# A state-space scan decimated by two, its sixteen tiles taken in eight pairs

## The chip, the cores and the metric

The kernel runs on one core of one Trainium2 chip. The metric is device time in microseconds (us) of the whole program, a network of two transformer-like layers and a third block. Everything is in float32.

## The reference, cut to what matters

The change touches one part of the first layer's mixer, the S5 scan. 32 groups of 64 complex states run over 256 time steps:

```python
lb = exp(a * dt)                                   # complex, |lb| = mag
bb = (lb - 1) / a * b                              # 16 inputs -> 64 states
bu = einsum('bsgc,gpc->bsgp', u, bb)
h[t] = lb * h[t-1] + bu[t]                         # by lax.associative_scan
y = real(einsum('bsgp,gcp->bsgc', h, c)) + d_skip * u
att = forgetting_attention(q, k, v, f_logit)       # 8 heads, softmax over 256 keys
y = gelu(y); y = y * sigmoid(y @ w_glu + b_glu)
out = concatenate([att, y]) @ w_out
```

## The kernel before, in words

The program has a thread per engine, written out by hand and held together by semaphores. Weights come in 1 MB units over SyncE's queue into a ring of twelve slots. In the first phase (class `Fox`) four of them are lent out as working memory, so that eight hold weights. Every VectorE, ScalarE and GpSimd instruction waits for the one before it (`Steps`).

In `Fox` the 32 groups are 16 tiles of 128 partitions (two groups of 64 states). Tile j runs through these steps:

- `tile_input` (L801, TensorE): two matmuls of 32 rows and 256 columns make the real and imaginary input in one PSUM bank (`INPUT`, banks 0 and 1).
- `turn_in` (L1155 to L1157, VectorE): the input is multiplied by a table of cosines and sines of -t times the state's angle, so that what is left is a real recurrence. The sum of the two products is GpSimd's (L1177).
- `scan` (L1166, VectorE): two real scans of 256 steps. VectorE turns tile j+1 in ahead of scan j, so that GpSimd's sum runs behind it.
- `turn_back` (L1193, L1194, GpSimd): two products of 512 elements with the table give `by_cos` and `by_sin`.
- `tile_output` (L812 to L815, TensorE): four matmuls of 256 columns, with 32 output columns each, one beside the other in the array's column groups.
- `keep_turn` (L835, ScalarE) copies the result, and after every fourth tile `tile_sums` (L824, TensorE) folds four of them, again side by side, into the output y; `y_keep` adds the skip term.

The table (256 columns for each of 16 tiles) is built by VectorE by doubling; ScalarE mirrors its half (`mirror`). TensorE meanwhile makes the products of u, q and k, and the product of v between the first tiles. Then a loop over tiles 3 to 15 follows on every engine. Behind eight of the tiles (`HEAD_BEHIND`) one attention head each is done: `turn_p` (L598), `head_out` (L606, L608) and `scores` (L588, L790) on TensorE, maxima on VectorE, exponentials on ScalarE. TensorE issues `tile_input(j + 4)` at the end of iteration j:

```python
for j in range(3, 16):
    self.tile_output(pe, j)
    ...
    if 7 <= j + 4 < 16:
        self.tile_input(pe, j + 4)
```

After the loop comes the product with the output weights (`mix_part`, L946), the GLU and the layer norm.

Of the kernel before, what the change touches and what calls it, by code (L numbers as in the profile page):

```python
# [12 lines left out]
ACT = mybir.ActivationFunctionType  # L13
# [4 lines left out]
P = 128  # L18
SEQ = 256
# [329 lines left out]
class Start(Phase):  # L349
# [36 lines left out]
    def sync_second(self, sp):  # L386

        net, io, fox = self.net, self.net.io, self.net.phase_objects[1]
        for n, dst in enumerate(fox.C):
            sp.dma_start(dst, io["s5_c"][n].rearrange("p (k n) -> p k n", k=16)).then_inc(fox.s("params_loaded"), 16)  # L390
# [335 lines left out]
class Fox(Residual, Heads):  # L726
# [5 lines left out]
    HEAD_BEHIND = {5: 0, 6: 1, 8: 2, 9: 3, 10: 4, 12: 5, 13: 6, 14: 7}  # L732
# [4 lines left out]
    def __init__(self, net):  # L737
# [3 lines left out]
        self.uT = a.take(4 * SEQ, 4, SEQ)  # L741
# [4 lines left out]
        self.Cz = [a.take(512, 16, 32) for _ in range(2)]  # L746
        self.ut = a.take(1024)
        self.g = [self.ut[:, 0:512], self.ut[:, 512:1024], a.take(512)]
        self.t = a.take(512)
        self.w = a.take(20 * 16, 20, 16)  # L750
        self.ph = [a.take(16 * SEQ, 16, SEQ) for _ in range(2)]

        b = Arena(net.ring, self.LENT * UNIT)
        odd = [b.take(512) for _ in range(2)]
        self.C = [h.rearrange("p (a b) -> p a b", a=16) for h in odd]
        self.alloc_heads(b)
        self.sel = b.take(8 * P, 8, P, rows=8)
        self.ft = [b.take(SEQ, rows=8) for _ in range(6)]
        self.c_rows = b.take(16, NT, 8)
        self.strips = [b.take(SEQ) for _ in range(3)] + [a.take(SEQ)]  # L760
        self.f_strips = self.strips[0]
        self.turned = [[b.take(512) for _ in range(2)], odd]
        self.yT = self.catT[:, 4:8, :]
        self.mask = net.causal[:, :]
        self.sig = [self.B[0].rearrange("p a b -> p (a b)"), self.B[1].rearrange("p a b -> p (a b)")]

# [29 lines left out]
    def tile_input(self, pe, j):  # L796

        k, m = divmod(j, 4)
        t = self.net.T.open(pe, ("bu", j), self.INPUT)
        for part in range(2):  # L800
            mm = pe.matmul(t[:, part * SEQ:(part + 1) * SEQ], self.B[part][32 * m:32 * m + 32, k, :],  # L801
                           self.uT[32 * m:32 * m + 32, k, :], start=True, stop=True)
        self.net.T.close(("bu", j), mm)

    def tile_output(self, pe, j):

        T = self.net.T
        t = T.open(pe, ("turn", j), self.TURN)
        pe.wait_ge(self.s("h_ready"), j + 1)
        by_cos, by_sin = self.turned[j % 2]  # L810
        re, im = slice(0, SEQ), slice(SEQ, 2 * SEQ)
        pe.matmul(t[0:32, re], self.Cz[0][:, j, :], by_cos[:, re], start=True, stop=True, skip_group_check=True)  # L812
        pe.matmul(t[32:64, re], self.Cz[1][:, j, :], by_cos[:, im], start=True, stop=True, skip_group_check=True)
        pe.matmul(t[64:96, re], self.Cz[1][:, j, :], by_sin[:, re], start=True, stop=True, skip_group_check=True)
        T.close(("turn", j), pe.matmul(t[96:128, re], self.Cz[0][:, j, :], by_sin[:, im], start=True, stop=True,  # L815
                                       skip_group_check=True))

    def tile_sums(self, pe, k):

        T = self.net.T  # L820
        t = T.open(pe, ("y", k), self.SUMS)
        pe.wait_ge(self.s("turn_kept"), 4 * k + 4)
        for m in range(4):
            mm = pe.matmul(t[32 * m:32 * m + 32, 0:SEQ], self.net.fold[:, 0:32], self.strips[m], start=True, stop=True,  # L824
                           skip_group_check=True)
        T.close(("y", k), mm)

    def keep_turn(self, act, j):

        net, T = self.net, self.net.T  # L830
        k, m = divmod(j, 4)
        if k:
            T.take(act, ("y", k - 1))
        t = T.take(act, ("turn", j))
        net.ac(act.activation(self.strips[m], t[:, 0:SEQ], ACT.Copy, scale=self.w[:, 19, 0:1]))  # L835
        T.free(act, ("turn", j))
        act.sem_inc(self.s("turn_kept"), 1)

    def tensor(self, pe):
# [5 lines left out]
        pe.wait_ge(self.s("params_loaded"), 16 * 4)  # L845
        pe.wait_ge(self.s("u_kept"), 4)
        for j in range(2):
            self.tile_input(pe, j)
# [4 lines left out]
        self.tile_input(pe, 2)  # L853
        vs = [net.use_unit(pe) for _ in range(2)]
        t = T.open(pe, ("fox_v", 0), rest)
        net.part(pe, t, vs, net.xT, 0, range(4))
        self.tile_input(pe, 3)
        self.tile_output(pe, 0)
        T.close(("fox_v", 0), net.part(pe, t, vs, net.xT, 0, range(4, KT)))
        self.tile_input(pe, 4)  # L860
        self.tile_output(pe, 1)
        t = T.open(pe, ("fox_v", 1), rest)
        net.part(pe, t, vs, net.xT, 1, range(4))
        self.tile_input(pe, 5)
        self.tile_output(pe, 2)
        T.close(("fox_v", 1), net.part(pe, t, vs, net.xT, 1, range(4, KT)))
        net.release([u for u, _ in vs], ("fox_v", 1))
        self.tile_input(pe, 6)
        pe.wait_ge(self.s("c_ready"), 1)
# [7 lines left out]
        for j in range(3, 16):  # L877
            self.tile_output(pe, j)
            if j == 3:
                self.scores(pe, 1)  # L880
# [2389 lines left out]
```

## Time and profile before

| what | value |
|---|---|
| median of 3 runs | 1944.28 us (1937.16 to 1944.61) |
| the profiled execution's own time | 1941.67 us |
| its span, first to last instruction | 1939.5 us |
| TensorE busy | 1799.3 us, 93% of the span |
| VectorE, ScalarE, GpSimd busy | 563.7, 371.9, 209.9 us |
| mean granted TensorE clock | 0.961 |

A profile shows one execution. Times are us from the span's start. "Busy" leaves out waits; the rows of a timeline merge neighbours of a kind (x4), and in brackets stands how long the engine was idle before. PEld is the loading of weights into TensorE's array. In float32 a matmul of the program shows as two MATMUL records, so that "x4" of L801 is one tile's two matmuls. Where matmuls follow one another, the difference of two starts is the time that the first took; the durations themselves overlap.

### The profile page before, as it was taken

Reading aid. Unit: us, or ns where it says so; the run is one execution under the profiler, and the core shown is the slowest. Engines: PE = TensorE matmul, PEld = TensorE weight load, DVE = VectorE, ACT = ScalarE, POOL = GpSimd, SP = SyncE. Lnnn points to the kernel's source line nnn. Section 1 sums busy time; section 2 is a strip of 40 time slices with the busy share of each in tenths; the row PEclk is TensorE's granted clock in tenths of the full one; section 3 lists DMA queues with packets and bytes.
Section 4 is the critical chain, followed back from the end, with each engine's and each line's share of the span. In section 5 each row is a group of like instructions: output and inputs, shape, how many; then the busy total and the mean of one; then the engine's idle time right before and its main releaser. Section 6 shows DMA issues by size and latency. Waiting matters only on the chain.

```text
span 1939.5 us, 21648 instructions
## 1 busy us (share of the span) xinstructions
PE 1799.3 (93%) x6956; PEld 934.2 (48%) x6957; DVE 563.7 (29%) x1236; ACT 371.9 (19%) x679; POOL 209.9 (11%) x403
## 2 busy tenths in 40 slices
PE   8998799899989989999989999999999988888886
PEld 6444333486633337855865475444443333232332
DVE  8882500587650031431372221011140000000002
ACT  1233311222221111032241100111032111110101
POOL 0561122000002310000000000000001110110100
PEclk9858899999989989999999999999999999999998
DMA  9002499676428993323413344332357999999995
GB/s 376 23 1 97 187 377 422 262 278 243 174 89 321 422 405 133 149 111 141 174 55 123 131 158 151 153 130 98 144 226 293 422 422 422 422 422 422 422 422 248
DMA packets 70439, 468.82 MB, mean 242 GB/s; under 512 B 7848, under 2 KB 12112, under 8 KB 15072
## 3 DMA queue, kind: packets, MB, share of 16 engines
q1 hardware_dynamic: 66016, 457.56, 58.1%
q10 hardware_dynamic: 4352, 10.35, 1.6%
q8 instruction: 40, 0.66, 0.1%
q14 instruction: 31, 0.25, 0.0%
HBM read 466.82 MB, written 1.06 MB: 241 GB/s over the span
## 4 chain that ended last, share of the span: by engine, by line
PE 67%; DMA 18%; DVE 10%; issue 2%; ACT 2%; SPq 0%; POOL 0%; DVEq 0%; ACTq 0%; POOLq 0%
PE bank L255 18%; DMA ring_sb<-stream 17%; PE bank L268 13%; PE bank L2705 10%; PE bank L1667 4%; PE bank L2748 4%; PE bank L2715 4%; PE bank L2642 2%; DVE scratch_sb L1027 2%; PE bank L301 2%; PE bank L946 1%; PE bank L1945 1%; DVE scratch_sb L1166 1%; DMA scratch_sb<-before 1%; PE bank L1302 1%
## 5 line engine op out<-in xcount | busy, mean ns | idle before, releaser
L2705 PE MATMUL bank<-ring_sb,scratch_sb 128*64 128x512 f32 x1536 | 347.3, 600 | 55.0 <-DMA ring_sb<-stream 48.8
L268 PE MATMUL bank<-xT_sb,ring_sb 128*128 128x256 f32 x1216 | 264.3, 379 | 0.0
L2705 PEld LDWEIGHTS bank<-ring_sb,scratch_sb 128*64 128x64 f32 x1536 | 115.4, 138 | 282.3 <-issue 273.2
L268 PEld LDWEIGHTS bank<-xT_sb,ring_sb 128*128 128x128 f32 x1216 | 230.6, 190 | 33.5 <-issue 2.5
L255 PE MATMUL bank<-ring_sb,xT_sb 128*128 128x512 f32 x416 | 179.4, 592 | 0.0
L255 PE MATMUL bank<-ring_sb,scratch_sb 128*128 128x512 f32 x384 | 167.7, 598 | 7.3 <-ACTq L2309 3.9
L2748 PE MATMUL bank<-ring_sb,scratch_sb 128*64 128x512 f32 x768 | 171.9, 596 | 0.0
L2866 DVE TENSOR_TENSOR scratch_sb<-scratch_sb,bank 128x256 f32<-128x256 f32 (+1 forms) x32 | 17.7, 554 | 408.9 <-PE bank L2705 278.7
L255 PEld LDWEIGHTS bank<-ring_sb,xT_sb 128*128 128x128 f32 x416 | 78.9, 190 | 97.7 <-issue 97.6
L2715 PE MATMUL bank<-scratch_sb 128*128 128x512 f32 x256 | 123.7, 606 | 0.0
L255 PEld LDWEIGHTS bank<-ring_sb,scratch_sb 128*128 128x128 f32 x384 | 73.1, 191 | 98.5 <-issue 90.6
L2982 ACT ACTIVATE scratch_sb<-bank 128x256 f32<-128x256 f32 (+1 forms) x96 | 47.1, 491 | 379.6 <-PE bank L2730 203.1
L2910 POOL COPY scratch_sb<-scratch_sb 128x256 f32 x128 | 45.2, 397 | 537.9 <-PEq L2608 525.7
L2871 DVE COPY scratch_sb<-bank 128x512 f32<-128x512 f32 x32 | 22.1, 692 | 277.7 <-PE bank L2748 277.7
L2748 PEld LDWEIGHTS bank<-ring_sb,scratch_sb 128*64 128x64 f32 x768 | 52.3, 137 | 96.8 <-issue 96.8
L1667 PE MATMUL bank<-ring_sb,xT_sb 128*128 128x512 f32 x192 | 84.5, 592 | 0.0
L2918 POOL TENSOR_SCALAR scratch_sb<-iota_sb,scratch_sb 128x64 f32<-128x64 f32 x128 | 71.7, 578 | 0.2
L2715 PEld LDWEIGHTS bank<-scratch_sb 128*128 128x128 f32 x256 | 43.5, 190 | 56.6 <-issue 56.6
L1667 PEld LDWEIGHTS bank<-ring_sb,xT_sb 128*128 128x128 f32 x192 | 36.3, 190 | 42.0 <-issue 41.6
L2985 ACT ACTIVATE scratch_sb<-bank 128x256 f32<-128x256 f32 (+1 forms) x32 | 15.7, 491 | 202.3 <-PE bank L2705 202.3
L2642 PE MATMUL bank<-scratch_sb 128*128 128x512 f32 x96 | 47.9, 663 | 6.8 <-DVEq L2813 6.8
L1361 DVE SCALAR_TENSOR_TENSOR scratch_sb<-ring_sb,mod_sb,scratch_sb 128x512 f32<-128x512 f32 x56 | 42.1, 752 | 2.9 <-DVE scratch_sb L667 0.2
(405 smaller groups left out, 1743.9 us busy)
## 6 DMA issues: line engine op xcount, KB each, us to landing
ring_sb<-stream SPq DMA_DIRECT2D x432, 1024.0 KB, 10.8
rows_sb<-rows ACTq DMA_DIRECT2D x12, 512.0 KB, 4.8
xT_sb<-xT SPq DMA_DIRECT2D x2, 512.0 KB, 7.1
x_sb<-x SPq DMA_DIRECT2D x1, 1024.0 KB, 19.9
scratch_sb<-bias_by_distance ACTq DMA_DIRECT2D x1, 1024.0 KB, 5.3
out<-x_sb ACTq DMA_DIRECT2D x2, 512.0 KB, 2.6
scratch_sb<-decay ACTq DMA_DIRECT2D x1, 768.0 KB, 5.4
small_sb<-small SPq DMA_DIRECT2D x1, 640.0 KB, 13.7
```

Source lines behind the costliest of these rows:

```text
L255: mm = pe.matmul(t[:, :], actT[:, k, i * P:(i + 1) * P], w[:, k % 4, :], start=k == 0, stop=k == kt - 1)
L268: mm = pe.matmul(t[:, m * SEQ:(m + 1) * SEQ], w[:, k % 4, n0:n0 + P], actT[:, k, :], start=k == 0, stop=k == kt - 1)
L301: mm = pe.matmul(bank[:, :], actT[:, k, i * P:(i + 1) * P], w[:, k % 4, :], start=k == 0, stop=k == kt - 1)
L1361: net.dv(dve.scalar_tensor_tensor(part, w[:, k, :], c, part, ALU.mult, ALU.add))
L1667: mm = pe.matmul(self.gate_bank[:, :], net.xT[:, kk, i * P:(i + 1) * P], w[:, k, :], start=kk == 0, stop=kk == KT - 1)
L2642: return pe.matmul(bank[:, :], self.src[:, i, k * P:(k + 1) * P], self.pick[i], start=i == 0, stop=i == 1)
L2705: mm = pe.matmul(t[e * TILE:(e + 1) * TILE, :], self.xs[e][:, kk, :], ws[e][:, k, :], start=kk == 0, stop=kk == KT - 1, skip_group_check=True)
L2715: pe.matmul(T.bank[2 * i + c][:, :], self.scatter[:, i * P:(i + 1) * P], self.y[:, c * 512:(c + 1) * 512], start=False, stop=False, skip_g ...
L2748: mm = pe.matmul(T.bank[6 + c][e * TILE:(e + 1) * TILE, :], self.hidT[:, ff, e * TILE:(e + 1) * TILE], ws[e][:, f, c * 512:(c + 1) * 512], ...
L2910: pool.tensor_copy(self.xs[e][:, 4 * m:4 * m + 4, :], self.xg[:, 4 * m:4 * m + 4, bass.ds(at[e] + tile * TILE, TILE)])\
L2918: pool.tensor_scalar(self.weigh[:, i, e * TILE:(e + 1) * TILE], self.net.iota[:, tile * TILE:(tile + 1) * TILE], self.of_pair[:, 0, i, e:e ...
L2982: act.activation(out, src, ACT.Copy).then_inc(self.tile_sem(f"freed{b}", over), 1)
```

## The change

Every second step of the recurrence is left out: h[2n+1] follows from h[2n-1] with lb squared and the input lb*b*u[2n] + b*u[2n+1]. So a scan runs over 128 steps and gives the odd times. The output at odd times is C h as before, and at even times it is (C lb) h[2n-1] plus a direct term K0 u[2n] with K0 = C b. Two tiles that were of 256 steps are taken together as a pair with the same 512 elements.

- New weights: lb*b (`lag`), C (`Cz`) and C lb (`E`) are computed by VectorE in a compact form (16 columns for each tile, in place of 32), spread by ScalarE into block form (`spread`, 16 instructions), and TensorE turns lb*b by 32 matmuls (`lag_weights`) and computes K0 by 32 matmuls of 32x32 (`direct_weights`). `lag_weights` stands ahead of q's product and waits for the spread, `direct_weights` behind it.
- The table has 128 columns for each tile, so the doubling has one round fewer.
- `turn_in`, the sum and `turn_back` work on a pair with the element counts of a tile before. `scan` is four scans of 128 in place of two of 256.
- `pair_input` is 8 matmuls of 128 columns, all on the same 32 rows; `pair_output` 16 matmuls of 128 columns; `pair_sums` is done for every pair: two matmuls of 256 and two of 128 columns, all into the same 32 output partitions.
- In the loop `pair_input(p + 2)` stands ahead of the head in iteration p.
- The s5 parameters come in six transfers in place of four, with the same bytes.

```diff
-    HEAD_BEHIND = {5: 0, 6: 1, 8: 2, 9: 3, 10: 4, 12: 5, 13: 6, 14: 7}
+    HALF = SEQ // 2
+    MID = SEQ // 4
+    HEADS_BEHIND = ((), (0,), (1,), (2,), (3,), (4,), (5,), (6, 7))
...
+    def pair_input(self, pe, p):
+
+        t = self.net.T.open(pe, ("bu", p), self.INPUT)
+        for odd in range(2):
+            k, m = self.tile(p, odd)
+            rows = slice(32 * m, 32 * m + 32)
+            for part in range(2):
+                at = (2 * odd + part) * self.HALF
+                out = t[:, at:at + self.HALF]
+                pe.matmul(out, self.LB[part][rows, k, :], self.uT[rows, k, 0, :], start=True, stop=False,
+                          skip_group_check=True)
+                mm = pe.matmul(out, self.B[part][rows, k, :], self.uT[rows, k, 1, :], start=False, stop=True,
+                               skip_group_check=True)
+        self.net.T.close(("bu", p), mm)
...
+        for odd in range(2):
+            k, m = self.tile(p, odd)
+            rows = slice(32 * m, 32 * m + 32)
+            pe.matmul(t[rows, odd * SEQ:(odd + 1) * SEQ], self.net.fold[:, 0:32],
+                      self.strips[p % 2][:, odd * SEQ:(odd + 1) * SEQ], start=True, stop=False, skip_group_check=True)
+            mm = pe.matmul(t[rows, odd * SEQ:odd * SEQ + self.HALF], self.K0[rows, k, :], self.uT[rows, k, 0, :],
+                           start=False, stop=True, skip_group_check=True)
...
+        self.lag_weights(pe)
         pe.wait_ge(net.sem("strips_kept"), 1)
         net.small_T(pe, "fox_f", self.f_strips, 0, banks=rest)
         net.product_T(pe, "fox_q", net.xT, banks=rest)
+        pe.wait_ge(self.s("params_loaded"), 16 * 6)
+        pe.wait_ge(self.s("u_kept"), 4 + 2)
+        for p in range(2):
+            self.pair_input(pe, p)
+        self.direct_weights(pe)
         net.product_T(pe, "fox_k", net.xT, banks=rest)
...
+        for p in range(2, 8):
+            self.pair_output(pe, p)
+            self.pair_sums(pe, p - 1)
+            if p + 2 < 8:
+                self.pair_input(pe, p + 2)
+            for h in self.HEADS_BEHIND[p]:
+                self.turn_p(pe, h - 1)
                 if h >= 2:
                     self.head_out(pe, h - 2)
                 if h + 2 < HEADS:
                     self.scores(pe, h + 2)
...
         self.turn_in(dve, 0)
+        for p in range(8):
+            if p + 1 < 8:
+                self.turn_in(dve, p + 1)
+            self.scan(dve, p)
```

TensorE in the loop before, an iteration with a head (L812 to L815 the tile's output, L598 `turn_p`, L588 and L790 `scores`, L801 the input of the tile four further on):

```order
L812 MATMUL bank<-ring_sb,scratch_sb 32x256 [waits fox_h_ready,bank3_freed]
L813 MATMUL bank<-ring_sb,scratch_sb 32x256
L814 MATMUL bank<-ring_sb,scratch_sb 32x256
L815 MATMUL bank<-ring_sb,scratch_sb 32x256
L598 MATMUL bank<-ident_sb,ring_sb 128x128 [waits bank7_freed,head_p_ready]
L598 MATMUL bank<-ident_sb,ring_sb 128x128 x2
L588 MATMUL bank<-scratch_sb 128x128 [waits bank4_freed]
L790 MATMUL bank<-ring_sb 128x128
L588 MATMUL bank<-scratch_sb 128x256
L790 MATMUL bank<-ring_sb 128x256
L801 MATMUL bank<-scratch_sb 128x256 [waits bank0_freed]
L801 MATMUL bank<-scratch_sb 128x256
```

And now, iteration 3 up to the middle of the pair's input (L873 `pair_output`, L886 and L888 `pair_sums`, L852 and L854 `pair_input(5)`), which ends ahead of the head:

```order
L873 MATMUL bank<-ring_sb,scratch_sb 32x128 [waits fox_h_ready,bank3_freed]
L873 MATMUL bank<-ring_sb,scratch_sb 32x128 x15
L886 MATMUL bank<-ring_sb,fold_sb 32x256 [waits fox_turn_kept]
L888 MATMUL bank<-scratch_sb 32x128
L886 MATMUL bank<-ring_sb,fold_sb 32x256
L888 MATMUL bank<-scratch_sb 32x128
L852 MATMUL bank<-scratch_sb 128x128 [waits bank1_freed]
L854 MATMUL bank<-scratch_sb 128x128
L852 MATMUL bank<-scratch_sb 128x128
L854 MATMUL bank<-scratch_sb 128x128
```

The input moved from four tiles ahead, behind the head, to two pairs ahead, in front of it, and the sums stand in every iteration.

VectorE now, from the turn-in of a pair (L1268 to L1270; `bank0_ready` is its input from TensorE) to the scans of the pair before it (L1284):

```order
L1268 TENSOR_TENSOR scratch_sb<-bank,scratch_sb 128x512 [waits vector_steps,fox_cleared,fox_h_ready,bank0_ready,fox_table_ready]
L1269 TENSOR_TENSOR scratch_sb<-bank,scratch_sb 128x2x128 [waits vector_steps]
L1270 SCALAR_TENSOR_TENSOR scratch_sb<-bank,scratch_sb 128x2x128 [waits vector_steps]
L1284 SCALAR_TENSOR_TENSOR scratch_sb<-scratch_sb 128x128 [waits vector_steps,fox_cleared]
L1284 SCALAR_TENSOR_TENSOR scratch_sb<-scratch_sb 128x128 [waits vector_steps] x3
```

The scans of pair p stand behind the turn-in of pair p+1, as those of tile j did behind tile j+1.

## Rows read from the trace of the kernel before

**Rows 1.** The page's first line.
```profile
span 1939.5 us, 21648 instructions
```

**Rows 2.** Busy time by window: PE, PEld, DVE, ACT, POOL, then granted clock, DMA share, GB/s.
```profile
57.90:85.50 27.60, 27.56 (x94) 12.00 (x94) 22.53 (x28) 4.15 (x7) 19.80 (x16) 0.88 0.07 28
85.50:143.50 58.00, 55.22 (x213) 28.12 (x210) 48.30 (x79) 21.95 (x59) 34.66 (x28) 0.50 0.00 1
143.50:161.30 17.80, 12.30 (x66) 5.53 (x64) 8.44 (x16) 9.74 (x27) 7.43 (x6) 0.69 0.01 1
```

**Rows 3.** SyncE's queue in order of time: start, duration, instruction.
```profile
25.25 176.11 SPq L3019 DMA_DIRECT2D ring_sb<-stream  x17
```

**Rows 4.** VectorE in order of time: start, duration, line, shapes, idle before.
```profile
56.18 0.69 DVE L1155 TENSOR_TENSOR scratch_sb<-bank,scratch_sb 128x512 f32<-128x512 f32 x1 [0.22 <-DVE ring_sb L1028]
...
69.40 0.69 DVE L1155 TENSOR_TENSOR scratch_sb<-bank,scratch_sb 128x512 f32<-128x512 f32 x1 [0.25 <-DVE scratch_sb L1166]
...
70.59 0.42 DVE L1157 SCALAR_TENSOR_TENSOR scratch_sb<-bank,scratch_sb 128x256 f32<-128x256 f32 x1
71.26 2.80 DVE L1166 TENSOR_TENSOR_SCAN scratch_sb<-scratch_sb 128x256 f32<-128x256 f32 x2 [0.24 <-DVE scratch_sb L1157]
```

**Rows 5.** GpSimd in order of time, the same tile.
```profile
70.63 1.26 POOL L1194 TENSOR_TENSOR ring_sb<-scratch_sb 128x512 f32<-128x512 f32 x1
72.08 1.43 POOL L1171 TENSOR_TENSOR scratch_sb<-scratch_sb 128x512 f32<-128x512 f32 x1 [0.18 <-POOL ring_sb L1194]
```

**Rows 6.** The scan's line: shortest, median, longest of its 32 instructions in ns.
```profile
L1166 DVE TENSOR_TENSOR_SCAN scratch_sb<-scratch_sb x32: 691/1208/1809, 61.7 to 152.8; 128x256 f32<-128x256 f32 x32
```

**Rows 7.** TensorE in order of time, at the full clock.
```profile
71.30 1.12 PE L801 MATMUL bank<-scratch_sb 32*128 32x256 f32 x4
72.36 0.40 PE L812 MATMUL bank<-ring_sb,scratch_sb 128*32 128x256 f32 x1
...
82.87 0.48 PE L588 MATMUL bank<-scratch_sb 64*128 64x128 f32 x2
83.28 0.48 PE L790 MATMUL bank<-ring_sb 8*128 8x128 f32 x2
```

**Rows 8.** TensorE in order of time, at half the clock.
```profile
130.30 0.90 PE L598 MATMUL bank<-ident_sb,ring_sb 128*128 128x128 f32 x3
131.13 1.12 PE L606 MATMUL bank<-ring_sb,scratch_sb 128*64 128x256 f32 x2
...
132.60 0.79 PE L588 MATMUL bank<-scratch_sb 64*128 64x128 f32 x2
133.33 0.79 PE L790 MATMUL bank<-ring_sb 8*128 8x128 f32 x2
...
137.20 0.64 PE L812 MATMUL bank<-ring_sb,scratch_sb 128*32 128x256 f32 x1
...
138.21 2.07 PE L801 MATMUL bank<-scratch_sb 32*128 32x256 f32 x4
140.21 0.64 PE L812 MATMUL bank<-ring_sb,scratch_sb 128*32 128x256 f32 x1
...
141.06 0.65 PE L824 MATMUL bank<-ring_sb,fold_sb 128*32 128x256 f32 x3
...
142.08 0.90 PE L598 MATMUL bank<-ident_sb,ring_sb 128*128 128x128 f32 x3
```

**Rows 9.** The chain that ended last: start, duration, what.
```profile
59.39 6.61 PE bank L301 x8
...
72.99 3.63 PE bank L301 x8
...
161.34 9.42 PE bank L946 x18
```

**Rows 10.** TensorE in order of time, the products of q and k.
```profile
27.75 27.89 PE L268 MATMUL bank<-xT_sb,ring_sb 128*128 128x256 f32 x128
```

**Rows 11.** ScalarE in order of time, the copy ahead of the added spreads.
```profile
26.29 0.38 ACT L288 ACTIVATE ring_sb<-bank 128x256 f32<-128x256 f32 x1 [0.65 <-PE bank L281]
```

More of the change, by code:

```diff
@@ L818, in tile_sums @@
-    def tile_sums(self, pe, k):
-        T = self.net.T
[L821 to L828, printed above, removed]
-        net, T = self.net, self.net.T
[L831 to L836, printed above, removed]
+            t = T.open(pe, ("lag", part), self.STATE)
@@ new lines, in pair_sums @@
+    def pair_sums(self, pe, p):
+        T = self.net.T
+        key = ("y", p // 4)
+        t = T.bank[T.jobs[key][0]] if p % 4 else T.open(pe, key, self.SUMS)
+        pe.wait_ge(self.s("turn_kept"), p + 1)
+        for odd in range(2):
+            k, m = self.tile(p, odd)
+            rows = slice(32 * m, 32 * m + 32)
[3 more added lines that the diff above has]
+                           start=False, stop=True, skip_group_check=True)
+        if p % 4 == 3:
+            T.close(key, mm)
@@ L851, in tensor @@
         net.product_T(pe, "fox_q", net.xT, banks=rest)
-        net.product_T(pe, "fox_k", net.xT, banks=rest)
[L853 to L868, printed above, removed]
+        pe.wait_ge(self.s("params_loaded"), 16 * 6)
[3 more added lines that the diff above has]
+        self.direct_weights(pe)
+        net.product_T(pe, "fox_k", net.xT, banks=rest)
+        self.pair_input(pe, 2)
         pe.wait_ge(self.s("c_ready"), 1)
@@ L873, in tensor @@
         T.close("fox_cT", mm)
-        pe.wait_ge(self.s("qkv_kept"), 6)
+        pe.wait_ge(self.s("qkv_kept"), 4)
         pe.wait_ge(self.s("sel_loaded"), 16)
         self.scores(pe, 0)
[L877 to L880, printed above, removed]
-            if j % 4 == 0:
-                self.tile_sums(pe, j // 4 - 1)
-            if j in self.HEAD_BEHIND:
-                h = self.HEAD_BEHIND[j]
-                if h >= 1:
-                    self.turn_p(pe, h - 1)
+        vs = [net.use_unit(pe) for _ in range(2)]
+        t = T.open(pe, ("fox_v", 0), rest)
+        net.part(pe, t, vs, net.xT, 0, range(4))
+        self.pair_output(pe, 0)
+        self.scores(pe, 1)
+        T.close(("fox_v", 0), net.part(pe, t, vs, net.xT, 0, range(4, KT)))
+        self.pair_input(pe, 3)
+        t = T.open(pe, ("fox_v", 1), rest)
+        net.part(pe, t, vs, net.xT, 1, range(4))
+        self.pair_output(pe, 1)
+        T.close(("fox_v", 1), net.part(pe, t, vs, net.xT, 1, range(4, KT)))
+        net.release([u for u, _ in vs], ("fox_v", 1))
+        self.pair_sums(pe, 0)
+        self.scores(pe, 2)
+        pe.wait_ge(self.s("qkv_kept"), 6)
+        for p in range(2, 8):
[5 more added lines that the diff above has]
+                self.turn_p(pe, h - 1)
                 if h >= 2:
@@ L1167, in scan @@
+    def scan(self, dve, p):
+        n = self.HALF
+        dve.wait_ge(self.s("cleared"), 1 + p + 1)
+        for odd in range(2):
+            for part in range(2):
+                at = (2 * odd + part) * n
+                xs = self.g[p % 3][:, at:at + n]
+                j = 4 * self.tile(p, odd)[0] + p % 4
+                mag = self.w[:, 0, j:j + 1].to_broadcast([P, n])
+                self.net.dv(dve.tensor_tensor_scan(xs, mag, xs, 0.0, ALU.mult, ALU.add))
         dve.sem_inc(self.s("g_ready"), 1)
@@ L1183, in turn_back @@
[L1183 to L1194 removed]
+        po = self.net.po
@@ new lines, in gpsimd, with turn_back @@
+        self.turn_back(pool, 7)
+    def turn_back(self, pool, p):
+        net, T, n = self.net, self.net.T, self.HALF
+        cr, ci = (table[:, self.tiles(p), :].unsqueeze(2).to_broadcast([P, 2, 2, n]) for table in self.ph)
+        g = self.pair_of(self.g[p % 3])
+        u, t = (v[:, :, 1:n + 1].rearrange("p (o a) n -> p o a n", o=2) for v in self.turned[p % 2])
+        pool.wait_ge(self.s("g_ready"), p + 1)
+        if p >= 2:
+            T.take(pool, ("turn", p - 2))
+        net.po(pool.tensor_tensor(u, g, cr, ALU.mult))
+        net.po(pool.tensor_tensor(t, g, ci, ALU.mult))
```

364 lines of the change are left out of this document (210 added, 154 removed).

## The prediction

> **What bounds the kernel now.** I read the page first, then the windows of the first 358 us, the chain of waits up to there, and the timelines of TensorE, VectorE, GpSimd and ScalarE in the first phase. The phase ends with the product that starts at 161.34 [rows 9]. From the first turn-in at 56.18 [rows 4] to the last scan behind 152.8 [rows 6] the chain runs through VectorE's turn-ins and scans. A scan alone takes 0.69 us and 1.81 us where GpSimd's sum runs beside it [rows 6], so work that lies side by side on the two engines is paid one after the other. TensorE is nearly as full: 55.22 of the 58 us from 85.5 to 143.5, at a granted clock of 0.50 [rows 2], the lower of its two levels (1.2 of 2.4 GHz). That is what the reader should see: VectorE sets the end, but TensorE is a few per cent behind it. The DMA queues do nothing in this phase (share 0.00 in the window); SyncE's queue stands from 25.25 for 176 us until slots come back [rows 3]. So whatever the phase gains or loses moves all that follows by the same amount, and nothing absorbs it.
>
> **What the change takes from VectorE and GpSimd.** A pair has the element counts of one tile, so there are 8 turn-ins, sums and turn-backs in place of 16, and scans half as long. If these engines still set the end, some 40 us would go. The work that prepares it (19 products on compact weights, one round of doubling less) ends near where it does now; TensorE's cover for it is over 15 us, since by the sum below it asks for the first pair's turn-back only at about 85, and that is ready near 76. I cost it at nothing. If that cover were gone, the path would be TensorE's K0, ScalarE's logarithm and the table's mirror, and the first turn-in would come 5 to 10 us later than now.
>
> **What it costs TensorE, one matmul at a time.** The stream of a 256-column matmul is 27.89/64 = 0.44 us at the full clock [rows 10], so 128 columns take 0.22, and 0.44 at half. An input matmul of 32 rows and 256 columns takes 1.06/2 = 0.53 [rows 7] and 2.00/2 = 1.00 at half [rows 8]. With 128 columns only the stream halves, which leaves 0.31 and 0.56; a 128-column matmul on 64 rows takes 0.41 [rows 7] and 0.73 [rows 8]. I take 0.36 and 0.62, so `pair_input` costs 8 x that, 2.9 and 5.0 us; the bounds are 0.27 and 0.41 (full), 0.50 and 0.73 (half). `pair_output` has the streams of two tile outputs, 0.63 each (72.36 to 72.99) [rows 7, 9] and 0.85 at half (140.21 to 141.06) [rows 8]: 1.1 and 1.9 with the change of shape; bounds 0.9 to 1.3 and 1.7 to 2.2. `pair_sums` is the part that loses most. Before, four folds ran side by side in 1.02 us for four tiles [rows 8]; now two folds (0.85 to 1.0 each at half) and two K0 matmuls (0.5 to 0.73) stand one behind the other for each pair: 2.9, and 1.7 at the full clock, bounds 2.7 to 3.4. A head is as before: from 130.30 to 132.60 `turn_p` and `head_out` 2.3, and scores 4.6 - 1.0 = 3.6, since 4.6 us to the next output hold an input of 2.0 of which part runs beside the scores [rows 8]; 5.9 in all at half, 3.4 at the full clock.
>
> **Ahead of the loop.** `lag_weights` waits for eight spreads behind 26.29 + 0.38, each 0.38 and a handover [rows 11]: 30.1. Lag matmuls 2.5 (bounds 1.8 and 3.5), the small product 0.6, q's product 13.95 (half of rows 10): 47.2. Two inputs, one at each clock, 7.9, and 32 tiny matmuls, 64 records at between 0.03 and 0.13 us, 4: 59.1. k's product 13.95 and 3 more, because dense work after sparse work starts at half the clock: v's first part took 6.61 where a later one took 3.63 [rows 9]. That is 76.1, against 55.6 now. The third input, the transpose and scores 0: 5.3, v in four parts 14.6 and again 3.0, two outputs 2.2, one sum 1.7, the fourth input 2.9, scores 1 and 2 4.2: the loop starts at 110.0.
>
> **The loop.** Here the change adds a wait. `pair_output(p+1)` needs scan p+1, which stands on VectorE behind the turn-in of pair p+2, and that needs `pair_input(p+2)`, which TensorE ends only in iteration p. From its end: handover 0.1, turn-in 1.6 (69.40 to 71.01), 0.24 to the scan [rows 4], four scans of 0.42 (0.69 shortened in proportion, with a fixed part of 0.16) and one of them held 1.12 by the sum [rows 6], 0.1 between each two and behind them in total 0.2, turn-back 2 x 1.26 and the gap [rows 5], 0.2 to TensorE: 7.8 us. The head of 5.9 runs meanwhile, so TensorE stands for 2 us in each iteration; queued behind its wait are the sums, the next input and the next head, and VectorE waits for that input. Iteration 2 up to its input is 1.9 + 2.9 + 5.0 = 9.8, to 119.8. Three more periods of 7.8 + 9.8 = 17.6 make 172.6. Then 7.8, output and sums 4.8, head 5.9, output and sums 4.8, two heads without scores 4.6, the last 2.3 and sums 2.9: 205.7. Outputs, sums and transposes alone gave the clock back in this trace (0.69 on average after 143.5) [rows 2], so I take off 3: 202.7, against 161.34. The phase is 41 us longer. Against the profiled execution's own 1941.67 us (span 1939.5 [rows 1]) that is **1983 us**. The median of the runs shown is 2.6 us above that execution; I leave the difference in the range.
>
> **A rule against the trace.** TensorE is busy 95% of the window 85.5 to 143.5 and yet has half the clock [rows 2]. The Trainium skill ("TensorE: Matmul & The Clock Gate", section "Why this matters for your kernels") says that a TensorE kept continuously busy gets the full clock. By the trace the loop stays at half, and the sum is 1983; by the rule TensorE would run it at full and the sum would be the first rival's. The measurement decides here, since this loop has the same kinds of small matmuls, and waits besides.
>
> **The rivals.**
> - Full clock: the two inputs and the three dense starts lose no time to the clock (110.0 becomes 101.9), 5.7 up to the input, three periods of 7.8 + 5.7, then 7.8 and 14.6: 170.5, or 9 us longer, **1951 us**. For it: 0.88 in the window with v's product [rows 2]. Against it: each period would have 4 us of standing still, and the loop before had 0.50 with almost none.
> - The other side, faster: the full clock throughout and weights loaded entirely behind streams, so that only columns count (pair input 1.75, output 0.9, sums 1.3). It decides at 0.22 us for a 128-column matmul. The loop starts at 93.7, comes to its input at 97.7, three periods of 7.4 + 3.95 make 131.7, and 7.4 and 13 end it at 152.1: 9 us shorter, **1932 us**. Against it: no row has a 128-column matmul with 128 columns of weights under 0.41. The 40 us of VectorE and GpSimd can't be had even so, as TensorE's own work alone ends here.
> - Dearer: inputs at 0.73 (0.8 more for each of six), sums 3.4, the tiny matmuls 8, half the clock also in the v stretch and at the end: 17 us more, **2000 us**.
>
> **How the numbers follow.** The forecast has 0.66, full clock 0.16, faster 0.06, dearer 0.12. The forecast's own range, from the bounds of the matmuls, is 1966 to 1996. With the full-clock case and most of the dearer one it is 1950 to 2004, which leaves out about 0.16. A measurement of this kernel can tell about 0.5% (10 us) from no change: below 1934.6 or above 1954. Faster 0.05 (most of the third case), the same 0.11 (the better part of full clock and the rest of the third), slower 0.84.
>
> **What the profile after should show.** The first L268 product ends near 47, the second near 76; L301 ends near 105; the loop's L873 groups come about 17 us apart at clock 0.50, each behind a wait for GpSimd of 1 to 3 us; VectorE's L1268 waits for TensorE's bank; eight L852 and L854 matmuls take 4.5 to 5.5 us; the mix product starts near 203. Prices under 0.3 us for L852 at full clock, or a clock near 1 in the loop, would make the forecast wrong; so would L873 without waits.

## The result: 0.55% slower, and the profile after

The changed kernel takes 1950.41 us in the median of seven runs (1948.42 to 1954.28), the kernel before 1941.78 (1936.27 to 1944.61) on the same chip: a ratio of 1.0055 (95% interval 1.0038 to 1.0072), 8.6 us more. The forecast was 41 us more, 1983 us; the measured time lies at the very edge of the range of 1950 to 2004. The profiled execution took 1949.64 us, its span is

```profile
span 1947.9 us, 22251 instructions
```

The windows of [rows 2] with the same columns, and a fourth up to the mix product:

```profile
57.90:85.50 27.60, 27.60 (x141) 18.47 (x140) 11.33 (x22) 2.92 (x5) 8.85 (x7) 0.94 0.11 39
85.50:143.50 58.00, 50.73 (x333) 29.60 (x332) 25.17 (x50) 17.68 (x45) 15.17 (x12) 0.74 0.00 1
143.50:161.30 17.80, 15.97 (x114) 9.09 (x113) 11.36 (x26) 7.54 (x20) 6.32 (x5) 0.71 0.01 2
161.30:175.40 14.10, 9.33 (x33) 4.08 (x31) 0.20 (x2) 5.72 (x15) 0.00 (x0) 0.64 0.00 0
```

From 85.5 to 143.5 VectorE went from 48.30 to 25.17 us and GpSimd from 34.66 to 15.17: the gain that the change aims at is there and lies beside the path. TensorE fell only from 55.22 to 50.73, at a granted clock of 0.74 where it was 0.50. (The window holds v's product at the full clock as well; in the three periods of the loop from 110.82 to 151.91 the clock is 0.62.) The chain that ended last (start, duration, what) has the products of q, k and v and then the mix product, at 161.34 before [rows 9]:

```profile
33.86 14.62 PE bank L268 x64
...
52.88 15.34 PE bank L268 x64
...
72.28 5.33 PE bank L301 x8
...
175.50 7.92 PE bank L1005 x18
...
231.18 16.61 PE bank L2763 x32
...
250.13 8.75 PE bank L2826 x32
```

So the phase is 14.2 us longer. One period of the loop on TensorE, in order of time, from one `pair_output` to the next:

```profile
124.52 1.93 PE L873 MATMUL bank<-scratch_sb 128*32 128x128 f32 x32 [1.89 <-POOLq L1316]
126.25 1.06 PE L886 MATMUL bank<-ring_sb,fold_sb 128*32 128x256 f32 x2
127.24 0.40 PE L888 MATMUL bank<-scratch_sb 32*32 32x128 f32 x2
127.57 0.62 PE L886 MATMUL bank<-ring_sb,fold_sb 128*32 128x256 f32 x2
...
128.45 0.48 PE L852 MATMUL bank<-scratch_sb 32*128 32x128 f32 x2
128.78 0.38 PE L854 MATMUL bank<-scratch_sb 32*128 32x128 f32 x2
129.00 0.38 PE L852 MATMUL bank<-scratch_sb 32*128 32x128 f32 x2
...
130.43 0.75 PE L599 MATMUL bank<-ident_sb,ring_sb 128*128 128x128 f32 x3
...
138.24 1.93 PE L873 MATMUL bank<-ring_sb,scratch_sb 128*32 128x128 f32 x32 [1.85 <-POOLq L1316]
```

Output 1.7 us, sums 2.2, input 2.0, then 7.8 from the end of the input to the next output, of which the head fills 5.9 and 1.85 is a wait for GpSimd. The clock changes twice in each period: the output and the first fold at half, the second fold and the input at full (starts 0.22 apart), the head at half again. The chain that fills the 7.8 us, on VectorE and then GpSimd, here in front of the output at 110.82, is the one forecast:

```profile
103.13 0.69 DVE L1268 TENSOR_TENSOR scratch_sb<-bank,scratch_sb 128x512 f32<-128x512 f32 x1 [4.84 <-PE bank L854]
103.86 0.42 DVE L1269 TENSOR_TENSOR scratch_sb<-bank,scratch_sb 128x256 f32<-128x256 f32 x1
104.32 0.42 DVE L1270 SCALAR_TENSOR_TENSOR scratch_sb<-bank,scratch_sb 128x256 f32<-128x256 f32 x1
104.98 2.91 DVE L1284 TENSOR_TENSOR_SCAN scratch_sb<-scratch_sb 128x128 f32<-128x128 f32 x4 [0.24 <-DVE scratch_sb L1270]
```
```profile
104.97 1.26 POOL L1299 TENSOR_TENSOR scratch_sb<-scratch_sb 128x512 f32<-128x512 f32 x1 [11.11 <-DVEq L1272]
108.03 1.26 POOL L1314 TENSOR_TENSOR ring_sb<-scratch_sb 128x512 f32<-128x512 f32 x1 [1.79 <-DVEq L1285]
109.37 1.26 POOL L1315 TENSOR_TENSOR ring_sb<-scratch_sb 128x512 f32<-128x512 f32 x1
```

Two more stretches of TensorE, ahead of q's product and the tail:

```profile
29.38 3.64 PE L817 MATMUL bank<-ident_sb,scratch_sb 128*32 128x128 f32 x64 [4.59 <-ACTq L1079]
...
162.77 0.38 PE L609 MATMUL bank<-ring_sb,scratch_sb 128*64 128x128 f32 x2
166.28 0.90 PE L599 MATMUL bank<-ident_sb,ring_sb 128*128 128x128 f32 x3 [3.12 <-ACTq L705]
...
170.29 0.90 PE L599 MATMUL bank<-ident_sb,ring_sb 128*128 128x128 f32 x3 [1.65 <-ACTq L705]
...
172.60 1.06 PE L886 MATMUL bank<-ring_sb,fold_sb 128*32 128x256 f32 x2
```

The lag weights wait 4.59 us for ScalarE's spreads, and behind the last pair two heads wait 3.12 and 1.65 us for ScalarE's weights, with the last sums behind them.

### The profile page after: what moved, and what is told of

It is laid out like the page before. It is cut to its first block, busy times and chain, and to the rows that moved or that the text cites. A ratio compares the mean times of both kernels' runs of the same rounds, so it can differ in the third digit from the quotient of the medians.

```text
span 1947.9 us, 22251 instructions
## 1 busy us (share of the span) xinstructions
PE 1800.3 (92%) x7308; PEld 945.5 (49%) x7309; DVE 528.5 (27%) x1218; ACT 376.2 (19%) x690; POOL 181.3 (9%) x384
## 3 DMA queue, kind: packets, MB, share of 16 engines
HBM read 466.82 MB, written 1.06 MB: 240 GB/s over the span
## 4 chain that ended last, share of the span: by engine, by line
PE 71%; DMA 17%; DVE 6%; ACT 2%; issue 2%; POOL 1%; SPq 0%; ACTq 0%; DVEq 0%; POOLq 0%
PE bank L255 18%; DMA ring_sb<-stream 17%; PE bank L268 14%; PE bank L2826 10%; PE bank L1788 4%; PE bank L2869 4%; PE bank L2836 4%; PE bank L2763 2%; PE bank L301 2%; PE bank L1005 1%; PE bank L2066 1%; PE bank L1423 1%; PE bank L995 1%; PE bank L589 1%; PE bank L873 1%
## 5 line engine op out<-in xcount | busy, mean ns | idle before, releaser
L2826 PE MATMUL bank<-ring_sb,scratch_sb 128*64 128x512 f32 x1536 | 345.8, 597 | 56.0 <-DMA ring_sb<-stream 49.8
L2826 PEld LDWEIGHTS bank<-ring_sb,scratch_sb 128*64 128x64 f32 x1536 | 114.6, 137 | 282.3 <-issue 273.5
L2763 PE MATMUL bank<-scratch_sb 128*128 128x512 f32 x96 | 44.6, 624 | 6.8 <-DVEq L2934 6.8
```

Of the source, the lines that this page charges most:

```text
L2763: return pe.matmul(bank[:, :], self.src[:, i, k * P:(k + 1) * P], self.pick[i], start=i == 0, stop=i == 1)
L2826: mm = pe.matmul(t[e * TILE:(e + 1) * TILE, :], self.xs[e][:, kk, :], ws[e][:, k, :], start=kk == 0, stop=kk == KT - 1, skip_group_check=True)
```

## Experiments

Two theories. **Order:** the phase is longer because the change puts waits on TensorE: behind its own `pair_input(p+2)` in each iteration (3.52 + 1.89 + 1.85 + 1.83 = 9.1 us), for the spreads, and in the tail. **Clock:** TensorE's own work is the bound, and the waits only give it the clock that it would not have without them. A third was whether the prices of small matmuls explain it. All edits are against the changed kernel; ratios are against the kernel before, run on the same chip. Experiments 6, 7 and 10 have one execution each, so only their profiles are read.

**1. The input ahead of the output.**
```diff
 for p in range(2, 8):
+    if p + 2 < 8: self.pair_input(pe, p + 2)
     self.pair_output(pe, p)
     self.pair_sums(pe, p - 1)
-    if p + 2 < 8: self.pair_input(pe, p + 2)
```


> In the loop pair_input(p+2) is issued ahead of pair_output(p) in place of behind pair_sums(p-1). Theory A (order): the change costs time since TensorE waits in each iteration for a chain of 7.9 us that starts at the end of its own pair_input. The four waits in front of pair_output(3) to (6), 3.52 + 1.89 + 1.85 + 1.83 = 9.1 us, go, the mix product starts near 166.4 in place of 175.5 and the time falls by about 9 us. Theory B (clock): the waits are what gives TensorE its clock back; without them the loop runs at half, pair_input takes 4.0 us in place of 2.0 and the sums 2.9 in place of 2.2, so each period is about 14.6 in place of 13.7 us and the time rises by 3 to 4 us.

Ratio 1.0005 (0.9984 to 1.0026), a median of 1939.23 us within 1930.17 to 1949.61, and the mix product starts at 161.04. The waits for GpSimd that are left are 0.40 and 0.95 us. The clock did not fall:
```profile
85.50:143.50 58.00, 56.65 (x407) 34.52 (x405) 34.86 (x71) 22.75 (x59) 21.56 (x17) 0.82 0.00 1
```
Moving one call took 14.5 us off the phase and undid the slowdown. The waits account for 7.7 us of it (9.1 less the 1.35 left); most of the rest is the better clock (0.76 in place of 0.67 from the loop's first output to the mix product), which the order theory had not foreseen. The clock theory's loss did not come.

**2. The input between output and sums.**
```diff
     self.pair_output(pe, p)
-    self.pair_sums(pe, p - 1)
     if p + 2 < 8: self.pair_input(pe, p + 2)
+    self.pair_sums(pe, p - 1)
```


> In the loop pair_input(p+2) is issued between pair_output(p) and pair_sums(p-1); the same matmuls, only that the 2.2 us of sums now lie inside the chain of 7.9 us in place of ahead of it. Theory A: in each period the sums fill the wait: 1.85 us less three times and 2.2 once, 7.8 us less, with the waits for GpSimd down to nothing or a few tenths. Theory B: the input, now right behind the output at half the clock, takes 4 us in place of 2, and the gain is gone: within 1 us of the changed kernel.

Ratio 1.0087 (1.0072 to 1.0101), by the ratios 6 us slower than the changed kernel, though the two intervals touch at 1.0072; mix product at 175.67, as the clock theory expected. The waits are gone in the loop after its first, and the clock went with them; the whole period of 14.7 us (121.59 to 136.31) is dense and at half (0.50 in it):
```profile
85.50:143.50 58.00, 54.52 (x323) 32.29 (x322) 25.19 (x51) 17.68 (x45) 15.20 (x12) 0.66 0.00 1
```
```profile
121.59 1.94 PE L873 MATMUL bank<-scratch_sb 128*32 128x128 f32 x32
123.45 0.79 PE L852 MATMUL bank<-scratch_sb 32*128 32x128 f32 x2
...
127.16 1.06 PE L886 MATMUL bank<-ring_sb,fold_sb 128*32 128x256 f32 x2
...
130.27 0.90 PE L599 MATMUL bank<-ident_sb,ring_sb 128*128 128x128 f32 x3
...
136.31 1.08 PE L873 MATMUL bank<-ring_sb,scratch_sb 128*32 128x128 f32 x16
```
The input takes 3.7 us here in place of 2.0. The clock theory is right for this order; the order theory's 7.8 us were all eaten. Taking waits away is worth only what the clock leaves of it. Why the clock rose with the order of experiment 1 and fell with this one, no run shows.

**3. The input's matmuls twice** (pairs 4 to 7, each sum written a second time).
```diff
-        for odd in range(2):
+        for odd in (0, 1, 0, 1) if p >= 4 else (0, 1):
```


> The eight matmuls of pair_input are issued twice for pairs 4 to 7 (the second set writes the same sums again). Both theories: the work stands ahead of the chain, so all of it is paid: 1.75 us by the measured spacing of 0.22 us, four times, 7 us more. If weight loads were the price of these matmuls it would be over 8 us; at half the clock 14 us.

Ratio 1.0116 (1.0098 to 1.0134), some 12 us over the changed kernel in place of 7. The added matmuls start 0.22 us apart until the clock falls inside the second set, and the sums ahead of it take 2.9 us in place of 2.2: a period of 16.8 (112.52 to 129.33), 3.1 more for 1.75 of work at the full clock. The last of the four periods had its whole input at half and took 19.7 us, and the mix product of this execution, the slowest of the four (1968.99; the others 1960.31 to 1964.58), starts at 196.44. So work ahead of the chain is paid in full, and the clock adds to it.

**4. The transposes three times** (heads 0 to 4).
```diff
-        for b in range(3):
+        for b in list(range(3)) * (3 if self.tag == "fox" and g < 5 else 1):
```


> turn_p issues its three transposes three times for heads 0 to 4, some 1.4 us more of TensorE's work at half the clock in each iteration 2 to 6 (one of them, in iteration 2, ahead of the 3.5 us wait), all behind pair_input. Theory A: TensorE stands idle there for 1.8 us or more, so nothing is paid: within 1 us of the changed kernel, and the waits for GpSimd shrink to about 0.4. If TensorE's own work were the bound and the waits only seeming, five times 1.4, 7 us more.

The mix product starts at 174.71 (175.50 in the changed kernel), and the period is 13.7 us as before. So the wait chain sets when the next output starts, and not the head's work on TensorE. The wait did not shrink to 0.4 us, as expected, but grew to 2.15: the clock rose with the added work, from 0.74 to 0.82 in the window and from 0.62 to 0.75 in the three periods, and the head with its added transposes took less time than the head alone had (5.7 us against 5.9). So the run does not show work being hidden in the wait. Nor did the time stay within 1 us of the changed kernel: the ratio is 1.0078 (1.0064 to 1.0091), some 4 us more, though the intervals overlap. In this profile the mix's first 18 matmuls took 9.48 us, against 7.92 in that of the changed kernel.

**5. The changed kernel again.**

> The changed kernel itself, without an edit, beside the kernel before on the chip of the runs that follow. First reading: 1.0055 (1.0038 to 1.0072), with the phase 14.2 us longer. All theories: the phase ends again within 1.5 us of 175.5, since nothing in it is left to chance but the clock of TensorE. If later stages, whose instructions are the same in both kernels, only happened to get a better clock in the first reading, the ratio here comes nearer to 1.007; if they systematically give 5 us back, it stays at 1.0045.

Ratio 1.0057 (1.0037 to 1.0076). The mix product starts at 172.90, 2.6 us earlier, all of it before k's product ends (65.62 against 68.22); from there to the mix product both profiles have 107.28 us. The clock in the window is 0.72. So the first reading stands, though the start of the mix product was expected within 1.5 us of 175.5.

**6. The last sums in the tail's wait.**
```diff
     for h in self.HEADS_BEHIND[p]:
+        if h == HEADS - 1: self.pair_sums(pe, 7)
         self.turn_p(pe, h - 1)
...
 self.head_out(pe, HEADS - 2)
-self.pair_sums(pe, 7)
```


> pair_sums(7) is issued in iteration 7 between the groups of heads 6 and 7, ahead of the transposes of head 6, where TensorE waits 3.12 us for ScalarE; in the changed kernel it stands behind the last head and in front of the mix product. If the last stretch is a chain through ScalarE (weights of head 6 and 7) with TensorE waiting, the sums are hidden and the mix product starts 2.5 to 3.1 us earlier, near 172.7. If TensorE's work bounds the stretch, it starts where it did, near 175.5.

From the last output to the mix product 12.4 us (158.70 to 171.11), against 16.3 in the changed kernel (159.23 to 175.50): 3.9 less, where 2.5 to 3.1 were expected; the time was 1945.75 us. The first wait fell to 1.36 us, as the sums lie in it, and they and the transposes behind them ran at the full clock:
```profile
163.43 0.62 PE L886 MATMUL bank<-ring_sb,fold_sb 128*32 128x256 f32 x2
163.98 0.40 PE L888 MATMUL bank<-scratch_sb 32*32 32x128 f32 x2
165.75 0.55 PE L599 MATMUL bank<-ident_sb,ring_sb 128*128 128x128 f32 x3 [1.36 <-ACTq L705]
```

**7. The lag weights behind q's product** (ScalarE's last eight spreads go ahead of its copies of them).
```diff
-self.lag_weights(pe)
...
 net.product_T(pe, "fox_q", net.xT, banks=rest)
+self.lag_weights(pe)
```


> lag_weights moves from ahead of q's product to behind it; ScalarE does the spreads of Cz and E ahead of the copies of the lag weights. In the changed kernel TensorE waits 4.59 us for the spreads in front of lag_weights. If that wait is paid, the loop and the mix product come 3 to 4.6 us earlier (1.3 us for ScalarE's copies now stand in front of the first inputs), near 171.5. If something else holds the first outputs (the turn-back of pair 0 is ready 9.5 us before TensorE asks for it), still the same gain, since TensorE is the engine that is late. Rival: the clock takes it back, the sparse work now ahead of k's product costs its first microseconds at half, within 1 us of 175.5.

The wait of 4.59 us becomes 0.62 and 0.93 us, and the lag matmuls take 1.95 us where they took 3.64. k's product starts at 48.98 (52.88 and 51.61 in the two profiles of the changed kernel), but it takes 15.55 us, against 15.34 and 14.01. The mix product starts at 171.99, 3.5 and 0.9 us earlier; the time was 1946.26 us. The gain is real at k's start (3.9 and 2.6 us). Against the first profile nearly all of it stays, as expected; against the second, k's product gives 1.5 us of it back through the clock, as the rival said.

**8. Scan before turn-in**, the order undone on VectorE and GpSimd.
```diff
-            if p + 1 < 8: self.turn_in(dve, p + 1)
             self.scan(dve, p)
+            if p + 1 < 8: self.turn_in(dve, p + 1)
...
             pool.sem_inc(self.s("cleared"), 1)
-            if p: self.turn_back(pool, p - 1)
-        self.turn_back(pool, 7)
+            self.turn_back(pool, p)
```


> VectorE scans pair p before it turns pair p+1 in, and GpSimd turns pair p back before it sums pair p+1; TensorE's order is that of the changed kernel. So the part of the change that turns the next pair in ahead of each scan is undone. Theory A: that part is what ties pair_output(p+1) to pair_input(p+2); without it the chain to an output starts at an input that TensorE ended a whole iteration earlier, the waits of 3.52 + 1.89 + 1.85 + 1.83 us go (or fall to what 1.6 turn-in, 1.4 sum, 2.0 scans and 2.6 turn-back in series leave), and the mix product starts 6 to 9 us earlier, near 168, if the clock stays. Theory B (clock): without waits TensorE gets half, as with the input ahead of the sums (period 14.7): within 2 us of 175.5. If neither engine's order matters and GpSimd's rate is the bound, no change at all.

Ratio 1.0031 (1.0015 to 1.0046), 4.7 us under the changed kernel; the mix product starts at 169.50. TensorE does not wait at all in the loop:
```profile
85.50:143.50 58.00, 58.00 (x354) 34.32 (x353) 23.07 (x55) 18.73 (x48) 16.01 (x13) 0.72 0.00 1
```
The clock takes part of it back: the periods are 11.7, 14.6 and 11.7 us. This shows that the wait comes from the turn-in ahead of the scan, as the prediction had it. (One of its twelve executions took 3742 us, at a mean granted clock of 0.483, and is left out of the ratio; the others took 1941 to 1951. Its cause is open.)

**9. Four edits together:** 1, 7, the last sums ahead of the last head's transposes, and heads 5 and 6 behind pair 6 with only head 7 behind pair 7.

```diff
-    HEADS_BEHIND = ((), (0,), (1,), (2,), (3,), (4,), (5,), (6, 7))
+    HEADS_BEHIND = ((), (0,), (1,), (2,), (3,), (4,), (5, 6), (7,))
...
+        self.pair_sums(pe, 7)
         self.turn_p(pe, HEADS - 1)
         self.head_out(pe, HEADS - 2)
-        self.pair_sums(pe, 7)
```


> Four edits together: pair_input(p+2) ahead of pair_output(p), lag_weights behind q's product, heads 5 and 6 behind pair 6 and only head 7 behind pair 7, and pair_sums(7) ahead of the last head's transposes. From inputs_ahead (phase end 160.97): 3 to 4 us less from the lag weights, 3 us less from the sums, 1.5 to 2 us less from one wait for ScalarE fewer in the tail. The mix product starts near 152.5, 9 us ahead of the kernel before, the time is 0.5% under it: a ratio of 0.995. If the clock decides instead (dense small matmuls at half), the phase ends above 160 and the ratio is 1.000.

Ratio 0.9931 (0.9905 to 0.9956): faster than both kernels. Mix product at 150.87, waits in the tail 1.05 and 0.48.

**10. The same without the heads' edit**, which is the diffs of 1, 6 and 7.

> pair_input(p+2) ahead of pair_output(p), lag_weights behind q's product, pair_sums(7) ahead of head 6's transposes; the heads as in the changed kernel (6 and 7 behind the last pair). Against the four edits together (mix product at 150.87) it leaves out the heads' edit. If the heads' edit brought the tail's second wait, 1.65 to 3 us, this one starts the mix product at 152.5 to 154; if the gain of the four was mostly the clock that the tail happened to get, the start is within 1 us of 150.9.

Mix product at 152.66, in the range, and a time of 1931.33 us. The waits for ScalarE in the tail are 1.36 and 1.65 us, 1.5 more than in 9, which is most of the 1.8 us between the two profiles. But one profile of each does not show what the heads' edit is worth, since two executions of kernel 12 below are 10.7 us apart.

**11. The additional head behind pair 2.**
```diff
-    HEADS_BEHIND = ((), (0,), (1,), (2,), (3,), (4,), (5, 6), (7,))
+    HEADS_BEHIND = ((), (0,), (1, 2), (3,), (4,), (5,), (6,), (7,))
```


> As the four edits together, but the additional head stands behind pair 2 (heads 1 and 2) in place of behind pair 6. The work of TensorE is the same, so the sum of waits decides: behind pair 2 ScalarE's chain of two heads is 3 us longer than the gap that covers it, but the loop after it has one head of slack. Theory A: within 2 us of 150.87, ratio 0.993. If the early clock (full at the front) makes heads cheaper there, 1 us better; if the wait for head 2's weights is paid in full, 3 us worse.

Mix product at 149.36, ratio 0.9959 (0.9933 to 0.9985), not to be told from 9.

**12. The four edits of 9 and scan before turn-in** (the diffs of 9, 1, 7 and 8).

> The four edits and the order scan before turn-in. With pair_input already ahead of the output, the outputs no longer wait for the turn-in of the next pair but for 0.4 us or less, so theory A expects nothing from TensorE's side: within 1.5 us of 150.87. What it could bring is scans not held by GpSimd's sum (2.04 in place of 2.91 us for four); what it could cost is the series of sum and scan, 1.4 us per pair, on a chain that has 2 us of slack.

Ratio 0.9901 (0.9882 to 0.9920), the lowest found, 1% under the kernel before; the interval overlaps that of 9. But the profiled execution had the mix product at 154.84, not within 1.5 us of 150.87, with a clock of 0.68, and was its slowest (1929.34; the others 1918.8 to 1924.6).

**13. Does the clock fall out anew in each execution?** Three more profiles.

> The kernel with pair_input(p+2) ahead of pair_output(p), a second profile. Its times ranged over 19 us where the changed kernel's ranged over 7. If the clock falls out anew in each execution of the same loop, this profile has another clock in the window 85.5 to 143.5 than 0.82, and the mix product starts several us from 161.04, in step with the total. If the pattern belongs to the order, both are within 1.5 us and 0.03, and the spread of the times lies in later stages.

> A third profile of the same kernel, for the same question: clock per execution (mix start differs from 161.04 and from the second profile by over 2 us) against clock per order (all three within 1.5 us).

> The four edits and scan before turn-in, a second profile. Its first profile was its slowest run (1929.3 against a median of 1920.2) with the mix product at 154.84 and a clock of 0.68 in the window 85.5 to 143.5. If the clock falls out per execution, a run near 1920 has the mix product 4 to 9 us earlier, near 148, and a clock near 0.85; if not, it stays at 154.8 and the difference lies in later stages.

Input ahead of the output: mix product at 161.04, 162.05 and 156.58, clock 0.82, 0.79 and 0.88, time 1938.86, 1936.79 and 1930.65 us. Kernel 12: 154.84 and 144.15, in these windows (first and second profile):
```profile
85.50:143.50 58.00, 58.00 (x356) 35.55 (x354) 24.32 (x60) 22.23 (x58) 15.69 (x13) 0.68 0.00 1
```
```profile
85.50:143.50 58.00, 56.41 (x458) 33.78 (x458) 27.15 (x69) 30.17 (x79) 17.73 (x14) 0.91 0.00 1
```
The same instructions in the same order, 10.7 us apart in the phase and 10.9 in the time (1929.34 and 1918.44), both on one and the same chip, with the loop's first output at 95.57 and 96.23; on that chip too were the profiles with 162.05 and 156.58. The second profile of the input ahead of the output alone would have said the opposite, being within 1.5 us and 0.03 of the first; the third decided. In these orders the clock falls out per execution. In the changed kernel the course repeats to the hundredth of a microsecond from the end of k's product on, and its period hardly varies. What decides the clock of an execution was not found.

## Why the prediction was wrong in size

The direction, the place and the wait chain hold; the size is over by 27 us in the phase and 6 us behind it. Three steps of the prediction failed: that the loop stays at half the clock, the prices of the small matmuls, and that nothing behind the phase absorbs its length.

Experiment 2 divides the first two, since it has the output, the input and the sums of a period all at half: 8.7 us (121.59 to 130.27), where the forecast had 9.8 and the changed kernel took 5.9. So in each period prices were 1.1 us too high and the clock gave 2.8. Dividing the rows of the table up to the last input in this way, I estimate 16 us for the clock and 10 us for the prices; the 3.7 us from k's product to the loop are not divided.

| step | forecast, us | measured | off by |
|---|---|---|---|
| up to the end of q's product | 47.2 | 48.41 | +1.2 |
| two inputs | 7.9 | 3.4 | -4.5 |
| `direct_weights` | 4 | 1.05 | -3.0 |
| k's product | 16.95 | 15.34 | -1.6 |
| from there to the loop | 33.9 | 30.2 | -3.7 |
| iteration 2 up to the end of its input | 9.8 | 4.55 | -5.2 |
| three periods | 52.8 | 41.1 | -11.7 |
| from the last input to the mix product | 30.1 | 31.4 | +1.3 |
| start of the mix product | 202.7 | 175.5 | -27.2 |

- **VectorE and GpSimd at nothing:** right. Their 23 and 19 us of the window did not shorten the phase. The cover for the first turn-back was 9.5 us (ready at 68.1, asked for at 77.6), not over 15; the forecast's own times, 76 and 85, give 9.
- **The wait chain of 7.8 us:** right, 7.8 to 7.9. Four scans with one held take 2.91 us (sum: 2.8 + gaps), turn-back 2 x 1.26. That TensorE would stand for 2 us was right too (1.8 to 1.9; 3.5 the first time, where the head is shorter). That this comes from the added order is shown by 8 and 1, and that the chain, not the work beside it, sets the next output's start by 4.
- **The clock, "by the trace the loop stays at half":** this failed, and is the largest part. The periods ran at 0.62, with most of the sums and the whole input at the full clock. I took the 0.50 of [rows 2] as a property of these kinds of matmuls. Experiment 2 shows that the same matmuls can run a whole period at half, 13 that they can run most of it at full (0.90 from the loop's first output to the mix product in the second profile of kernel 12). The rival with the full clock had the period at 13.5 us (13.7 measured), the loop's start at 101.9 (98.4) and the time at 1951; I gave it 0.16. That it comes so near is luck: its inputs were too dear, its outputs too cheap, it had the mix product at 170.5 (175.5), and the later stages gave back what it missed. What was against it, 4 us of standing still per period, was also what no row had tested: before, TensorE had hardly stood still.
- **The price of a 128-column input matmul,** 0.36 at the full clock within bounds of 0.27 and 0.41: it is 0.22, below the lower bound, which the prediction had named as a sign against itself. The rows had the reason in them. A call of eight takes 1.98 us (128.45 to 130.43), which is 8 x 0.22 and 0.2; the call of two with 256 columns in [rows 7] took 1.06, which is 2 x 0.43 and 0.2; at half the clock 3.7 is 8 x 0.43 and 0.3, and the 2.0 of [rows 8] is 2 x 0.85 and 0.3. So the part above the streams stands once for each call, and I had charged it to each matmul. About half of it lies at either end of the call; what causes it is not shown. The clock gives 2.3 of the two inputs' 4.5 us, the price 2.2.
- **The 32 tiny matmuls at 4 us:** 1.05 us in all, 16 ns for each of 64 records, half of my lowest price of 0.03 us.
- **The tail:** 30.1 against 31.4 looks right and is not. The matmuls were cheaper (the last output took 1.0 us, not 1.9), and two waits for ScalarE of 3.12 and 1.65 us, which I had not seen, filled the place. I had summed TensorE's heads and sums without asking whether ScalarE could deliver two heads in a row.
- **`lag_weights` at 30.1 + 2.5:** the wait was right (start 29.38), the matmuls took 3.4 until the small product.
- **"Nothing absorbs it":** this failed too. SyncE's queue did move with the phase, as said, but of 14.2 us only 8.3 were left at the last product. The unchanged stages behind ran at a better clock: the mix's first 18 matmuls took 7.92 us at a clock of 1.00 (9.42 at 0.84 before [rows 9]); from the start of the mix product to the first L2826 it is 74.6 us against 77.8 (161.34 to 239.13); and a later group of L2763 took 14.02 at 1.00, where the same group (then L2642) took 17.03 at 0.82. The kernel before, then the changed one:
```profile
239.13 8.78 PE bank L2705 x32
...
567.83 17.03 PE bank L2642 x32
```
```profile
579.61 14.02 PE bank L2763 x32
```
The second profile of the changed kernel repeats this (11.6 us at the mix product, 5.9 at the end), the kernel of experiment 2 only in part (14.3 and 12.7, its group took 17.07). Why those stages get the better clock after this phase was not settled.

The rule of the Trainium skill ("TensorE: Matmul & The Clock Gate", section "Why this matters for your kernels"), that a TensorE kept continuously busy gets the full clock, does not hold for this loop, as far as the profile tells what is busy: the loop of experiment 2 was busy for 54.5 of 58 us and ran whole periods at half, that of experiment 8 was busy throughout and had 0.72, and kernel 12 was busy for 58.0 us at 0.68 in one execution and 56.4 us at 0.91 in another. But the trace of the kernel before was no better guide. Weighing it as "the rule or the trace" was the mistake; both levels had to be priced as an alternation, and the range around 1983 should have had the full-clock case as a near equal.

## What to carry to other kernels

When a change gives work back to an engine beside the bound one, look for what it makes the bound engine wait for: here one call, the next input moved ahead of the output, was worth 10 us, the whole loss. Work put into a wait can be free, as the last sums in experiment 6 were. A short wait behind two stages of another engine (two heads in a row) is found only by summing that engine's chain as well. Look whether the part of a price above the stream belongs to each matmul or to the call. Price small matmuls at both clocks in every stretch, and where a kernel's times spread over 1%, take a second profile before believing the first one's clock.

## What was not expected of the hardware

- Matmuls of 32 rows of weights and 128 columns start 0.22 us apart at the full clock and 0.43 at half, the time of their columns alone; loading 128 columns of weights for each costs nothing visible. The 0.53 for each with 256 columns in the kernel before [rows 7] is the same stream time with 0.2 us for the call.
- 32 matmuls of 128 rows, 32 columns and 32 output rows (64 records) took 1.05 us, 33 ns each, with four groups of output rows in turn.
- The granted clock of one loop, instruction by instruction the same, differed by 0.23 between two executions of kernel 12 (0.68 and 0.91) and moved the phase by 10.7 us; in the changed kernel's two profiles the loop's course repeated.
- Adding transposes ahead of a wait raised the granted clock of the three periods from 0.62 (in both profiles of the changed kernel) to 0.75, in one profile of experiment 4.
- A scan of 128 columns took 1.53 us where GpSimd's sum of 1.26 us started with it, and 0.42 us in all 32 cases of experiment 8, where the order keeps the two apart.
